# Hybrid decoder step on one core: the sums of the first two units' weight blocks and the adding of late squares go from VectorE to GpSimd; the last squares are folded by VectorE and GpSimd; the last scalings and stores are split anew

## The reference

```python
u = rmsnorm(h, norm_mix_g[l])
z = u @ w_in[l]                      # 2048 x 3584: q, k, v, recurrent branch, gate
attn = sliding_window_attention(...)
rec = rg_lru(conv(xr)) * gelu(gr)
mixed = concat([rmsnorm(attn, attn_out_g[l]), rmsnorm(rec, rec_out_g[l])])
h = h + mixed @ w_out[l]             # 2048 x 2048
hid = square(relu(rmsnorm(h, norm_mlp_g[l]) @ w_up[l]))   # 2048 x 8192
h = h + hid @ w_down[l]              # 8192 x 2048
y = rmsnorm(h, final_norm_g)
```

## Time and profile before

| what | us |
|---|---|
| median of 3 runs | 2146.15 (2144.62 to 2148.6) |
| the profiled execution, its own time | 2148.01 |
| its span from the first to the last instruction | 2145.9 |
| TensorE busy in the span | 2089.2 |
| VectorE busy | 1571.9 |
| ScalarE busy | 959.7 |
| GpSimd busy | 242.5 |

### The profile page before, as it was taken

How to read it: one execution, slowest core, us unless ns; L and a number is a source line. 1 busy time by engine, 2 the same in 40 slices (tenths; PEclk the granted TensorE clock), 3 DMA queues, 4 the chain that set the end, 5 groups by cost and what they waited for, 6 DMA issues and landing times.

```text
span 2145.9 us, 38442 instructions
## 1 busy us (share of the span) xinstructions
PE 2089.2 (97%) x15402; PEld 2057.3 (96%) x15402; DVE 1571.9 (73%) x2017; ACT 959.7 (45%) x1321; POOL 242.5 (11%) x188
## 2 busy tenths in 40 slices
...
DMA packets 90667, 296.55 MB, mean 138 GB/s; under 512 B 10448, under 2 KB 19192, under 8 KB 90232
## 3 DMA queue, kind: packets, MB, share of 16 engines
...
## 4 chain that ended last, share of the span: by engine, by line
PE 64%; DVE 2%; issue 1%; ACT 1%; POOL 0%; DMA 0%; POOLq 0%; SPq 0%; ACTq 0%; DVEq 0%
PE ps L1029 64%; DVE w_pair L2095 1%; ACT w_pair L1453 0%; DVE blk L2112 0%; PE ps L1088 0%; POOL stage L1758 0%; DMA blk<-w_mlp 0%; ACT quad L1439 0%; DVE w_t L2112 0%; PE ps L777 0%; DVE part L2161 0%; DVE stage L2134 0%; POOLq L2495 0%; POOL fin L1758 0%; DVE stage L2178 0%
## 5 line engine op out<-in xcount | busy, mean ns | idle before, releaser
L1029 PE MATMUL ps<-quad,w_pair 128*128 128x288 f32 x10752 | 1438.3, 296 | 25.0 <-DVE w_pair L2095 10.7
L1029 PEld LDWEIGHTS ps<-quad,w_pair 128*128 128x128 f32 x10752 | 1430.9, 189 | 31.7 <-issue 20.5
L1453 ACT ACTIVATE w_pair<-blk 128x1024 fp32r<-128x1024 f32 (+7 forms) x426 | 415.3, 975 | 625.6 <-PE ps L1029 501.7
L2095 DVE TENSOR_TENSOR w_pair<-blk,w_pair 128x1024 fp32r<-128x1024 f32 (+7 forms) x426 | 475.2, 1117 | 171.7 <-ACT w_pair L1453 171.2
L736 PE MATMUL ps<-xact,w_hi 128*128 128x288 f32 (+1 forms) x2816 | 497.5, 299 | 9.5 <-DVE xact L1828 8.3
L736 PEld LDWEIGHTS ps<-xact,w_hi 128*128 128x128 f32 x2816 | 417.1, 189 | 12.4 <-ACT xact L1131 8.3
L736 PE MATMUL ps<-xact,w_lo 128*128 128x288 f32 (+1 forms) x1408 | 302.4, 296 | 0.0
L736 PEld LDWEIGHTS ps<-xact,w_lo 128*128 128x128 f32 x1408 | 227.3, 189 | 0.0
L1117 ACT ACTIVATE w_hi<-w_raw 128x1024 fp32r<-128x1024 f32 x88 | 93.0, 1058 | 255.8 <-PE ps L736 223.5
L1623 POOL TENSOR_TENSOR w_lo<-w_raw,w_hi 128x1024 fp32r<-128x1024 f32 x60 | 148.4, 2476 | 261.9 <-ACT w_hi L1117 261.9
L1758 POOL TENSOR_TENSOR stage<-stage,fin_rb 128x576 f32<-128x576 f32 x4 | 5.5, 1407 | 1499.1 <-ACT fin_rb L1609 1499.1
...
## 6 DMA issues: line engine op xcount, KB each, us to landing
...
```

What stands on the lines that cost most here:

```text
L1029: ins = nc.tensor.matmul(ps[:, i, 0:HW], w[:, k, :], quad[:, slot, lo, X_OPERAND[i], :], start=sow and opens and j == quads[0] and step == ...
L1453: nc.scalar.activation(w_half(v, i, 0), w_operand(v, i), ACT.Copy).then_inc(wh_ready, 1)
L2095: v.tensor_tensor(w_half(u, i, 1), w_operand(u, i), w_half(u, i, 0).bitcast(F32), ALU.subtract).then_inc(wl_ready, 1)
```

## The change

At the turn, GpSimd makes the four weight sums of units 0 and 1, eight instructions of 128x1024 that VectorE made before, and adds the squares of tiles 12 to 15. From unit 2 on VectorE makes the sums as before. The order of the turn's steps on VectorE and ScalarE is written anew. At the end, GpSimd adds the squares of unit f = 6, VectorE folds after its last evacuation and adds three quarters of the last squares to the folded halves, so that TensorE has three column sums in place of six. ScalarE squares the last unit before it scales the tiles of f = 4 and 5. GpSimd scales five tile halves in place of six, VectorE one more, and ScalarE's queue issues the five stores of GpSimd's tiles.

```diff
 # sync
-        for half, f in ((1, 3), (1, 4), (1, 5), (1, 0), (1, 6), (1, 7), (1, 1), (0, 3), (0, 4), (1, 2), (0, 5), (0, 0),
-                        (0, 6), (0, 1), (0, 7), (0, 2)):
...
+        for k, (half, f) in enumerate(((1, 3), (1, 4), (1, 5), (1, 6), (1, 7), (0, 3), (0, 4), (0, 5), (0, 6), (0, 7), (0, 2))):
             b = 2 * half
+            sp.wait_ge(y_ready, k + 1)
             sp.dma_start(y_t[(f - 1) % DEPTH, :, b:b + 2, :], home(2 * UP - 1 + f)[:, b:b + 2, :]).then_inc(stored, 16)
 # tensor
         pe.wait_ge(fin_squared, 8)
         column_sums(fin_last[:, 0, :], 0, True)
-        pe.wait_ge(fin_summed, 1)
-        column_sums(fin_sum[:, 0, :], 0)
+        pe.wait_ge(fin_summed, 3)
         column_sums(fin_sum[:, 1, :], 1)
-        pe.wait_ge(fin_squared, 9)
-        column_sums(fin_last[:, 2, :], 1)
-        pe.wait_ge(fin_squared, 10)
-        column_sums(fin_last[:, 3, :], 1)
-        pe.wait_ge(fin_squared, 11)
-        column_sums(fin_last[:, 1, :], 0).then_inc(sums_ready, 1)
+        pe.wait_ge(fin_summed, 4)
+        column_sums(fin_sum[:, 0, :], 0).then_inc(sums_ready, 1)
 # scalar, turn (the head of it)
+        quad_high(1)
         diff_high(1)
-        quad_high(1)
+        gain_h(3)
+        w_round(0, 0)
         quad_high(2)
+        quad_high(3)
         diff_high(2)
-        gain_h(3)
         square_h(KT - 4, 0)
-        w_round(0, 0)
+        w_round(0, 1)
         diff_high(3)
-        quad_high(3)
         gain_late(4)
-        w_round(0, 1)
+        square_h(KT - 3, 1)
+        store_h(6)
         gain_late(5)
...
 # gpsimd
+        def w_sum(u, k):
+            width = len(window(u)) * P
+            if k == 0:
+                blk_wait(pool, u, 1)
+                pool.wait_ge(wl_ready, 7 * u + 1)
+                dst, a, b = w_block(u, 0), w_block(u, 0), w_block(u, 1)
+            elif k == 1:
+                blk_wait(pool, u, 2)
+                if u == 0:
+                    pool.wait_ge(slab_used, SLABS - 2)
...
+                pool.wait_ge(w_summed, 4 * u + 1)
+                dst, a, b = w_t2[:, 0:width], w_block(u, 0), w_block(u, 2)
+            elif k == 2:
+                pool.wait_ge(wl_ready, 7 * u + 2)
+                pool.wait_ge(w_summed, 4 * u + 2)
+                dst, a, b = w_block(u, 3), w_t2[:, 0:width], w_block(u, 3)
+            else:
+                dst, a, b = w_block(u, 1), w_block(u, 1), w_block(u, 2)
+            nc.gpsimd.tensor_tensor(dst, a, b, ALU.add).then_inc(w_summed, 1)
...
+        add_h(KT - 4, 0)
+        w_sum(0, 0)
+        add_h(KT - 3, 1)
+        w_sum(0, 1)
+        w_sum(0, 2)
+        w_sum(0, 3)
+        add_h(KT - 2, 0)
+        add_h(KT - 1, 1)
+        w_sum(1, 0)
+        w_sum(1, 1)
+        w_sum(1, 2)
+        w_sum(1, 3)
+
+        pool.wait_ge(fin_squared, 7)
+        pool.wait_ge(fin_added, 5)
+        nc.gpsimd.tensor_tensor(fin_acc[:, :, :], fin_acc[:, :, :], fin_sq[:, :, :], ALU.add).then_inc(fin_added, 1)
 # vector, end
+        fin_fold()
+        for k, (half, b) in enumerate(((1, 2), (1, 3), (0, 1))):
+            dve.wait_ge(fin_squared, 9 + k)
+            dve.wait_ge(fin_summed, 1 + k)
+            v.tensor_tensor(fin_sum[:, half, :], fin_sum[:, half, :], fin_last[:, b, :], ALU.add).then_inc(fin_summed, 1)
```

More of the change, by code:

```diff
@@ L1556, in _ @@
         quad_high(6)
-        diff_high(4)
+        gain_late(6)
+        quad_high(7)
+        square_h(KT - 2, 0)
         diff_high(5)
-        square_h(KT - 2, 0)
-        quad_high(7)
         w_round(0, 3)
@@ L1609, in _ @@
             nc.scalar.activation(fin_rb[:, half, :], ps[:, FIN_BANKS[half][1], 0:HW], ACT.Copy).then_inc(fin_rb_ready, 1)
+        for k, (half, f) in enumerate(((1, 0), (1, 1), (1, 2), (0, 0), (0, 1))):
+            b = 2 * half
+            act.wait_ge(y_pool_ready, k + 1)
+            act.dma_start(y_t[(f - 1) % DEPTH, :, b:b + 2, :], home(2 * UP - 1 + f)[:, b:b + 2, :]).then_inc(stored, 16)
     @block.gpsimd
@@ L1755, in _ @@
             r = fin_rb[:, half:half + 1, :].to_broadcast([P, 2, HW])
-            for f in range(3):
+            for f in range(2 + half):
                 y = home(2 * UP - 1 + f)[:, 2 * half:2 * half + 2, :]
@@ L2105, in w_sum @@
                 blk_wait(dve, u, waits)
-            if u == 0 and k == 1:
-                dve.wait_ge(slab_used, SLABS - 2)
+            if u == 2 and k == 0:
+                dve.wait_ge(w_summed, 8)
             if k in (0, 2):
@@ L2284, in add_rec @@
             add_scaled(i, i % 2, h_tile(m), h_ready)
-        def add_square(m):
-            dve.wait_ge(h_squared, m + 1)
-            dve.wait_ge(h_added, m)
-            v.tensor_tensor(acc[:, META:T], acc[:, META:T], sq[:, m % 2, META:T], ALU.add).then_inc(h_added, 1)
         for m in range(KT - TURN, KT):
             add_att(m)
+        quad_low(1)
         diff_low(1)
-        quad_low(1)
         quad_diff(2)
-        quad_low(2)
-        add_rec(KT - 4)
-        diff_low(2)
-        quad_diff(3)
-        w_rest(0, 0)
-        w_sum(0, 0)
-        w_sum(0, 1)
-        add_rec(KT - 3)
+        w_rest(0, 0)
+        diff_low(2)
+        add_rec(KT - 4)
+        add_rec(KT - 3)
+        quad_diff(3)
+        w_rest(0, 1)
+        quad_low(2)
         quad_low(3)
+        base_sum(6)
+        add_rec(KT - 2)
         diff_low(3)
-        add_square(KT - 4)
         quad_diff(4)
-        base_sum(6)
-        w_rest(0, 1)
         quad_diff(5)
-        w_sum(0, 2)
-        w_sum(0, 3)
+        add_rec(KT - 1)
         quad_low(4)
         w_rest(0, 2)
-        add_rec(KT - 2)
         quad_low(5)
-        add_rec(KT - 1)
         quad_low(6)
         diff_low(4)
-        diff_low(5)
         quad_low(7)
```

44 lines of the change are left out of this document (16 added, 28 removed).

## The result

| | before | after |
|---|---|---|
| median | 2144.62 us (7 runs, 2142.77 to 2152.78) | 2155.53 us (7 runs, 2154.29 to 2157.57) |
| profiled execution, its own time | 2148.01 | 2157.57 |
| its span | 2145.9 | 2155.5 |

The ratio is 1.0047 with a 95% interval of 1.0036 to 1.0059, that is +10.1 us, between 7.7 and 12.7. The forecast was +13.5.

The account below looks back on a forecast made before the run. The prediction took VectorE, for which TensorE waits, as the full engine of the turn. Its terms 13.0 (turn) + 0.8 (clock) - 0.3 (end) = +13.5 us on 2146.15 gave 2159.7 us, range 2150 to 2166.

Parts of the forecast that it names:

- (1): Sign in the trace: VectorE instructions of 0.45 to 0.75 us take 2 to 3 us beside GpSimd's of 2.4 us.
- (2): Sign at the turn: TensorE goes on at 655 us, then waits some 10 us from 658 for `w_pair`.
- (3): Sign in unit 1: TensorE has a second wait of some 6 us at the spread of the norm.
- (5): Sign at the end: one `w_pair` instruction of nearly 3 us, and stores at the same GB/s.
- (4): Sign from unit 2 to the last but one: both kernels alike, shifted by 12 to 14 us.
- The first gap (+6.2): Step-by-step walk of the turn's start up to product 2: GpSimd's instructions delay VectorE's, costing 6.2 us.
- The rest of the turn (+6.5): Turn behind its first gap: 12.4 us of GpSimd work less 5.9 us spared on VectorE, +6.5 us.
- part of it: Rival: the first gap costs 6.2 us, but unit 1's sums fall while VectorE waits for ScalarE; 2152 us, chance 12%.
- the balance (24.8 - 11.8 us): At the turn: GpSimd's added 24.8 us less VectorE's spared 11.8 us, +13.0 us of VectorE time, an upper bound.
- The clock (+0.8): At the turn: a second gap at the diagonals brings the low clock again, +0.8 us, between 0 and 1.6.
- The end (-0.3): End phase: `w_pair` stands for GpSimd's add, while fewer column sums end sooner; -0.3 us, bounds -1.5 and +1.5.

Follow-up runs that it names:

- e2: The changed kernel with only unit 1's four weight sums back on VectorE: 2155.22 us, ratio 1.0053 to the kernel before.
- e1: The changed kernel with all eight weight sums of units 0 and 1 back on VectorE: 2150.45 us, ratio 1.0029 to the kernel before.
- e7: The changed kernel with all the turn's sums and squares on VectorE, leaving the new order and new end: 2151.15 us, ratio 1.002 to the kernel before.
- e9: The kernel before's order at the turn, with the changed kernel's GpSimd work and end: 2153.61 us, ratio 1.0037 to the kernel before.
- e6: The kernel before with the turn's steps on VectorE and ScalarE re-ordered another way, no work moved: 2144.23 us, ratio 0.9994.
- e11: e6 run again unchanged for a second profile: 2141.76 us, a single execution.
- e10: The kernel before with e6's order and the changed kernel's end: 2140.09 us, ratio 0.9975.
- e8: The kernel before, without an edit, run again for its second profile: 2144.89 us, a single execution.
- e3: The kernel before plus ten idle two-input adds on GpSimd at the turn, results read by nobody: 2160.88 us, ratio 1.008.

## Why the prediction came out

**The direction and the main mechanism were right, the sum 3.4 us too high, and a part of its size was met by luck.** The +13.5 lies just above the measured interval of 7.7 to 12.7. By the five points that it said would show it: (1) holds, 2.54 and 2.48 us for L2097 and L2099, and 0.46 with GpSimd idle. (2) holds, TensorE goes on at 655.97 and waits 9.95 us for `w_pair`. (3) holds, 5.93 us at the spread. (5) holds, 2.61 us and 383 GB/s. (4) holds at first: against the first profile of before, unit 2 is 13.7 us late, 1.1 of it from ahead of the turn. But the shift falls to 9.2 by unit 30. That is the pace of that one profile (last section). Against before's second profile the whole span is 12.8 us longer: 2.2 ahead of the turn (before's own two profiles differ by 1.1 there), 12.4 in the turn and -1.9 at the end. The last two make 10.5, which fits the +10.1 of the times.

**The first gap (+6.2).** Product 2 starts at 669.24 with 24 matmuls done. TensorE's wait there is 9.95 us against 4.52, +5.4. The walk was right to 0.8 us.

**The rest of the turn (+6.5).** The waits behind the first are 0.87, 0.53, 0.48 and 5.93 us, 7.8 in all, against 0.88, 0.25 and 1.09 in before's second profile, 2.2: +5.6. The size was nearly right, its make-up was not. I had put 5.0 of it down to unit 1's sums on GpSimd. With them on VectorE (e2) the turn is 1.2 us shorter and the wait at the spread 2.3. They cost less than I had, and not for the reason that the rival *part of it* gave: while GpSimd makes them, from 691.69 to 702.20 us, VectorE idles some 0.5 us only and its steps do stretch (a `w_pair` to 3.41, three of the chain to 0.91, 2.24 and 2.33); but its four instructions from 695.08 to 696.49 read PSUM or a single input and keep their 0.15 to 0.44 us beside a sum of 3.17. The rest of that wait, 3.6 of 5.93 us, is there with all sums on VectorE (3.58 in e1 and e7), and by the lists it is the later place of `diagonals`; no run moves that step alone. That a term of +6.5 met +5.6 was luck: part of its cause was too dear and a part was missing. So the rival's 2152 did not come either.

**The order, costed at nothing.** The prediction walked the new order through the first gap, and so had its effect there inside the 6.2; it gave no price to the order by itself. That later `diagonals` delays the spread, it put at nothing. e7 puts 8.0 us on the order without GpSimd, e9 and the changed kernel 1.9 us beside GpSimd's work. What I called the balance (24.8 - 11.8 us) is an upper bound, as it said: e9 measures 10.7.

**The clock (+0.8).** The first 48 matmuls behind the wait take 8.20 us where e6's take 6.57, and the 48 behind the spread 8.15 against 6.62 for 48 at the higher clock, 3.2 us together; before's second profile has 12.11 - 9.72 = 2.4 us of this kind and its first 1.6. So +0.8 against the one, as taken, and +1.6 against the other, the upper bound. Here two runs of one program differ too: behind the same 2.83 us of idle the granted clock from 662 to 668 us was 1.00 in e6 and 0.72 in e11.

**The end (-0.3).** The stand of `w_pair` came as costed. Of the column sums I took the kernel before at the end of its one profile, which was a short one: +0.3 against that, -1.9 against the second. This term and the turn's 1.3 us are most of the 3.4 us. The rest is within what the medians can tell.

## What to carry to other kernels

Work given to GpSimd is not taken off VectorE if both read SBUF: compare GpSimd's whole time (24.8 us here) with what VectorE is spared (11.8), and look which of VectorE's instructions have two inputs in SBUF, since one with an input in PSUM goes on undisturbed. It is cheap only where VectorE stands anyway. Before work is moved at all, look at the order in the queues: here `add_rec(14)` further ahead, and a few steps with it, gave 3.5 to 4.6 us in the traces without any work moved, while the changed kernel's order cost 8.0 us with all the turn's work on VectorE, three quarters of the 10.7 that the work on GpSimd cost. By the traces an instruction at the head of VectorE's list that waits for a slab has a part in that, and a short chain with a later place, `diagonals`, a larger one.

## What the runs showed beside this

**Two paces of the same code.** TensorE is busy without a pause in both, at the full granted clock, and needs 22.29 us for an upward unit in two of the fourteen profiles (the first of before and e10's) and 22.13 in the others. The windows of before in its first profile, then its second (the number in brackets counts the matmuls):

```profile
800.00:1000.00 200.00, 200.00 (x1509) 1.00 0.41 137
...
1600.00:1800.00 200.00, 200.00 (x1521) 1.00 0.51 175
```

```profile
800.00:1000.00 200.00, 200.00 (x1520) 1.00 0.39 134
```

From unit 40 to unit 70 all fourteen take 599 to 600 us. The slower pace costs 28 x 0.16 = 4.5 us and changes with the execution and not with the kernel, since before and e8 are one program. It may be a part of why times of one kernel lie up to 10 us apart: e10's profile at the slower pace is of an execution 3.8 us above its median. That isn't shown. I did not find the cause of the two paces. Whoever compares two single profiles finds it as a shift that slowly comes or goes far from the change.

**Turns, one by one.** GpSimd and VectorE alternate instruction by instruction, so a chain of short dependent instructions on VectorE suffers most: 2.24 us for one on five columns, where e3's 288-column ones took 1.95 in place of 0.46. In e9, with `diagonals` at its old place, the whole chain takes 7.9 us between unit 1's sums, against 2.3 before.
